# Six edits to a two-layer hybrid backbone: raw merge gates, weights' low parts ahead of the masks, gate matmuls between row transposes, squares added on VectorE, a shorter rotary

## Chip, cores and metric

The kernel runs on one core of a Trainium2 chip. The metric is device time in microseconds (us) of one execution; several executions are taken and their median is compared.

## What is computed

Two layers over 512 tokens of 1024 features (256 context tokens, then 256 latent ones); batch 1; all in float32. Layer 1 needs its context only as keys and values, so most of its work covers the 256 latent tokens.

```python
h  = rms_norm(x, g1) * (1 + sc) + sh          # modulation from c, by w_mod
p  = split(h @ w_in)                          # mLSTM | MLA | NA | three gates of 1024
y_a = mlstm(p)      # 4 heads x 2 directions, log-sigmoid gates, sums and maxima along time
y_b = mla(p)        # 8 heads, 64 plain + 32 rotary features, RMS-normed q and k
y_c = natten(p)     # 8 heads, windowed with a bias, plus the context
y  = (sigmoid(ga)*y_a + sigmoid(gb)*y_b + sigmoid(gc)*y_c) @ w_out
x  = x + g1 * y
x  = x + g2 * (square(relu(rms_norm(x) mod @ w_ff1)) @ w_ff2)
```

A sigmoid is taken as (1 + tanh(z/2)) / 2, where z is the output of the gate projection.

## The kernel before

**Precision.** Every weight and every activation of a large product is split in a high part and a low part (high by ScalarE, L832 for weights; low = raw - high by GpSimd, L693 and L695, or by VectorE, L1253, for a fixed share of the blocks). A product is three matmuls: high x high, low x high, high x low. Weights stream by SyncE's DMA into a raw buffer and pass through a ring of high and low places. `reach(n)` (L479) gives the block up to which places are free once block n has been used; `ahead(n)` (ScalarE, L837), `low_to(reach(n))` (GpSimd, L700) and `share_ahead(n)` (VectorE, L1244) make the parts up to there. Each engine runs its instructions in the order in which the program issues them, so the place of these calls in each engine's code is the schedule.

**Order of a layer.** Norm; the mLSTM's projection (blocks `ml`, seven); the mLSTM; neighbourhood attention (`na`); the latent attention (`mla`); the merge of three gated branches; output projection (`wo`); norm; the feed-forward pair (`ff`, 32 steps). The 24 tiles of the gate projections (`gate`, each 24 matmuls, L1881) are spread as filler: `chain` tiles while VectorE works on the mLSTM's scans, eight `loop` tiles in the loop over heads and directions, `last` tiles behind it, others (`cn`, `units`) in the preparation of the latent attention. `FILL` (L152) says how many where; `pump(tile, n)` (L1887) issues n matmuls of a tile.

**Gates.** `gate_out` (ScalarE, L843) takes a finished tile from its bank: with Tanh for the tiles before the `units` part, with Copy for those (`untouched`, L156). Some go to DRAM and come back by SyncE (`load_gate`, L571). `normed` (L965) needs a logarithm and an exponential for each head; ScalarE loads a function table where the next function is not in the one that it holds. `branch_out` (VectorE, L1540) multiplies 1 + tanh with a branch's output tile; in the latent attention two buffers (`side_tanh`) hold gates in turn.

**mLSTM.** After the last projection TensorE transposes small rows (L2009, L2014; L1370 and L1372 are VectorE's copies between them) and runs the chain tiles. VectorE computes for both directions (L1377 to L1399, four partitions wide) the gate sums and maxima by scans (L1389, L1392, L1394), and TensorE turns the result back (L2021, L2022). In the loop over `it` (L2060, 8 turns: 4 heads x 2 directions) it broadcasts a maximum (`broadcast_max`, L2030) for the next turn, which needs ScalarE's exponentials of this one (L962), runs 12 and 12 matmuls of a gate tile around the next head's scores (L2042), then, once GpSimd's mask (L731) is there, the products with the values (L2078). GpSimd's code is mask 0, low parts, mask 1, low parts, and so on. The last head is turned (L2053) after the last but one of the `last` tiles.

**Attentions.** Two heads or rows in each step s: VectorE takes the maxima (L1679), ScalarE the exponentials with their sums (L1136), VectorE or GpSimd divides (L1656, L763), TensorE transposes (L2228), ScalarE copies (L1155), TensorE multiplies with the values. Between these run the branch projection's matmuls (L1907). `rope` (L1327) is the rotary part: a multiply with the cosine (L1335), four small ones with the sine (L1339), an addition (L1341); a small copy (L1606) signals that a query block is done.

**Norm.** ScalarE squares each of eight chunks of the residual stream (L879); TensorE sums all of them over the partitions by a float32 matmul with ones (L1946, `square_sum`), two behind each residual chunk pair; ScalarE takes Ln and Exp (L891, L892); VectorE and ScalarE make the normed chunks, and the next projection begins (L1863).

```python
low_to(reach(N["ml", l, 6]))                       # GpSimd, ahead of the loop
for hd in range(2 * ML_H):
    pool.wait_ge(*S(f"ml{l}_P").at(hd + 1))
    pool.affine_select(...)                        # the mask, L731
    low_to(reach(N["gate", l, hd]))
```

## Time and profile before

| | us |
|---|---|
| median of three runs | 1687.56 (1683.96 to 1689.25) |
| the profiled execution, its own time | 1691.04 |
| its span, first to last instruction | 1689.3 |
| TensorE busy | 1576.3 |
| VectorE busy | 1000.5 |
| ScalarE busy | 757.5 |
| GpSimd busy | 691.4 |
| mean granted clock of TensorE | 0.970 of full |

The profiled execution is one more execution, taken with the hardware profiler. PE is TensorE, DVE is VectorE, ACT is ScalarE, POOL is GpSimd, SP is SyncE. A busy TensorE is not one at its peak, and the idle time of an engine off the bounding path costs nothing. Where several operations follow at one line, the timeline shows them as one row with their count.

### The profile page before, as it was taken

To read this page: it belongs to the slowest core of one execution; us is meant where nothing else is said; L and a number is where in the kernel's file an instruction comes from. 1 tells how busy PE (TensorE), PEld (TensorE's weight loads), DVE (VectorE), ACT (ScalarE), POOL (GpSimd) and SP (SyncE) were. 2 spreads that over 40 slices of the span, in tenths; PEclk is the share of its full clock that TensorE was granted. 3 is DMA by queue.
4 is the path that set the end of the run, shared out by engine and by line. 5 is a ranking of instruction groups with operands and counts; after the bars stand their busy time and mean duration, and the time that the engine had idled before them with its cause. 6 is when DMAs were issued, how large, how long until landed. Compare 5 with 4: busy or idle time off the path is not lost.

```text
span 1689.3 us, 24992 instructions
## 1 busy us (share of the span) xinstructions
PE 1576.3 (93%) x9728; PEld 1341.6 (79%) x9728; DVE 1000.5 (59%) x1737; ACT 757.5 (45%) x1506; POOL 691.4 (41%) x407
## 2 busy tenths in 40 slices
PE   7897998989999999899999998979898989989998
PEld 3776778967877687688888886967897876889998
DVE  5755934875367762668696964144127287665554
ACT  4424653455544643523232334347436545554443
POOL 0451324634343012455554543534455453234442
PEclk9998999999999999999999998989999999999999
DMA  8442434421225132243455742132520343435553
GB/s 328 185 183 81 181 113 150 151 100 53 83 100 193 26 128 97 75 159 122 169 199 193 279 151 100 69 100 81 162 101 26 122 144 101 157 129 192 179 178 122
DMA packets 69852, 230.64 MB, mean 137 GB/s; under 512 B 18280, under 2 KB 24808, under 8 KB 56424
## 3 DMA queue, kind: packets, MB, share of 16 engines
q1 hardware_dynamic: 60880, 213.67, 35.7%
q10 hardware_dynamic: 8856, 15.39, 2.5%
q8 instruction: 77, 1.26, 0.3%
q14 instruction: 39, 0.32, 0.1%
HBM read 216.45 MB, written 12.58 MB: 136 GB/s over the span
## 4 chain that ended last, share of the span: by engine, by line
PE 77%; DVE 9%; ACT 6%; POOL 4%; issue 3%; DMA 1%; ACTq 0%; DVEq 0%
PE bank L1843 39%; PE bank L1925 10%; PE bank L1881 8%; PE bank L1863 4%; PE bank L1907 3%; PE bank L2228 2%; PE bank L2204 2%; PE bank L2215 2%; POOL wL L693 1%; ACT wH L832 1%; POOL wL L695 1%; PE bank L2078 1%; DVE arena L1339 1%; DVE mjunk L1268 1%; PE bank L1946 1%
## 5 line engine op out<-in xcount | busy, mean ns | idle before, releaser
L695 POOL TENSOR_TENSOR wL<-raw,wH 128x768 fp32r<-128x768 f32 (+3 forms) x198 | 327.7, 1655 | 354.5 <-ACT wH L832 354.4
L832 ACT ACTIVATE wH<-raw 128x768 fp32r<-128x768 f32 (+6 forms) x396 | 296.9, 807 | 387.4 <-PE bank L1843 287.3
L693 POOL TENSOR_TENSOR wL<-raw,wH 128x1280 fp32r<-128x1280 f32 (+2 forms) x144 | 298.8, 2075 | 413.3 <-ACT wH L832 413.3
L1843 PE MATMUL bank<-hH,wH 128*128 128x512 f32 (+1 forms) x720 | 247.8, 344 | 2.4 <-POOL wL L695 1.5
L1843 PE MATMUL bank<-hH,wL 128*128 128x512 f32 (+1 forms) x720 | 244.6, 340 | 0.0
L1843 PE MATMUL bank<-hL,wH 128*128 128x512 f32 (+1 forms) x720 | 244.5, 340 | 0.0
L1843 PE MATMUL bank<-oH,wH 128*128 128x512 f32 (+1 forms) x576 | 194.5, 338 | 0.5 <-issue 0.5
L1843 PE MATMUL bank<-oH,wL 128*128 128x512 f32 (+1 forms) x576 | 193.6, 336 | 0.0
L1843 PE MATMUL bank<-oL,wH 128*128 128x512 f32 (+1 forms) x576 | 193.6, 336 | 0.0
L1271 DVE SCALAR_TENSOR_TENSOR acc<-acc,cb 128x1024 f32<-128x1024 f32 x88 | 167.2, 1914 | 2.5
L1881 PE MATMUL bank<-hH,wH 128*128 128x512 f32 (+1 forms) x384 | 138.8, 362 | 18.0 <-POOL wL L695 11.7
L1843 PEld LDWEIGHTS bank<-hH,wH 128*128 128x128 f32 x720 | 136.5, 190 | 19.9 <-POOL wL L695 2.1
L1843 PEld LDWEIGHTS bank<-hL,wH 128*128 128x128 f32 x720 | 136.6, 190 | 16.0 <-issue 1.2
L1843 PEld LDWEIGHTS bank<-hH,wL 128*128 128x128 f32 x720 | 136.5, 190 | 15.3
L1925 PE MATMUL bank<-wH,hH 128*128 128x256 f32 x480 | 138.9, 289 | 9.5 <-POOL wL L695 9.3
L1925 PE MATMUL bank<-wL,hH 128*128 128x256 f32 x480 | 137.7, 287 | 0.0
L1925 PE MATMUL bank<-wH,hL 128*128 128x256 f32 x480 | 137.6, 287 | 0.0
L1881 PE MATMUL bank<-hL,wH 128*128 128x512 f32 (+1 forms) x384 | 132.5, 345 | 0.0
L1881 PE MATMUL bank<-hH,wL 128*128 128x512 f32 (+1 forms) x384 | 132.4, 345 | 0.0
L1760 DVE SCALAR_TENSOR_TENSOR arena<-bank,modT,arena 128x256 f32<-128x256 f32 x120 | 54.1, 480 | 130.5 <-PE bank L1843 125.9
L1843 PEld LDWEIGHTS bank<-oH,wH 128*128 128x128 f32 x576 | 109.3, 190 | 12.5 <-issue 1.4
L1843 PEld LDWEIGHTS bank<-oL,wH 128*128 128x128 f32 x576 | 109.4, 190 | 11.6 <-issue 0.5
(213 smaller groups left out, 3140.7 us busy)
## 6 DMA issues: line engine op xcount, KB each, us to landing
raw<-in_p_ff SPq DMA_DIRECT2D x64, 1024.0 KB, 4.8
acc<-in_p_mod SPq DMA_DIRECT2D x44, 1024.0 KB, 5.4
raw<-in_p_ml SPq DMA_DIRECT2D x12, 1024.0 KB, 5.0
raw<-in_p_na SPq DMA_DIRECT2D x12, 1024.0 KB, 4.9
raw<-in_p_mgc SPq DMA_DIRECT2D x16, 512.0 KB, 3.5
raw<-in_p_mga SPq DMA_DIRECT2D x16, 512.0 KB, 3.5
raw<-in_p_mgb SPq DMA_DIRECT2D x16, 512.0 KB, 3.6
raw<-in_p_out SPq DMA_DIRECT2D x8, 1024.0 KB, 4.8
```

Of the source, the lines that this page charges most:

```text
L693: pool.tensor_tensor(l_[:, 0:cut], r_[:, 0:cut], h_[:, 0:cut].bitcast(F32), ALU.subtract)
L695: pool.tensor_tensor(l_[:, cut:k * w], r_[:, cut:k * w], h_[:, cut:k * w].bitcast(F32), ALU.subtract)\
L832: act.activation(flat(wH, n)[:, part], flat(raw, n)[:, part], ACT.Copy)\
L1271: ins = dve.scalar_tensor_tensor(row, row, 1.0, cb[:, last, :], ALU.mult, ALU.mult, accum_out=modT[:, l, chunk, last:last + 1])
L1760: ins = dve.scalar_tensor_tensor(x[:, c + b, lo:lo + 256], src[:, lo:lo + 256], modT[:, l, gate + c + b, s:s + 1], x[:, c + b, lo:lo + 256 ...
L1843: ins = pe.matmul(dst, w_[:, kk, c:c + P], r_[:, kk, lo:TOK], start=kk == k0 and m == 0, stop=kk == k0 + kn - 1 and m == 2)
L1863: ins = pe.matmul(dst, w_[:, kk, c:c + P], r_[:, kk, lo:TOK], start=kk == 0 and m == 0, stop=kk == KC - 1 and m == 2)
L1881: ins = pe.matmul(bank[gate_bank(l, T)][:, t0:TOK], w_[:, kk, :], r_[:, kk, t0:TOK], start=kk == 0 and m == 0, stop=kk == KC - 1 and m == 2)
L1907: ins = pe.matmul(bank[2 + T % 2][:, t0:TOK], w_[:, kk, :], r_[:, o + kk, t0:TOK], start=kk == 0 and m == 0, stop=kk == 3 and m == 2)
L1925: ins = pe.matmul(bk[:, o:o + width], s_[:, at[kk], t * P:t * P + P], w_[:, kk, c:c + width], start=kk == 0 and m == 0, stop=kk == k - 1 a ...
L2204: pe.matmul(bank[4 + i][:, 0:nk], l_q[0:MLA_D, 2 * g + i, t * P:t * P + P], l_k[0:MLA_D, 2 * g + i, 0:nk], start=True, stop=True).then_inc ...
L2215: ins = pe.matmul(bank[s % 2][64 * i:64 * i + 64, 0:P], v_[:, c, h * 64:h * 64 + 64], s_pt[:, i, c * P:c * P + P], start=c == 0, stop=c == ...
```

## The change

- `gate_out` always copies. The tanh is taken in the attentions by ScalarE (`branch_tanh`), in place, one step before `branch_out` needs it; `branch_out` waits for it. The reload of the logarithm's table in `normed` is taken out.
- GpSimd makes low parts up to the reach of the last chain tile before the first mask, and after mask hd those of the loop tile one turn earlier (none after mask 0).
- The first chain tile uses bank 2 and is issued in pieces: 5 matmuls (8 in layer 1) before the row transposes of L2009, 4 (6) before those of L2014, the rest behind. Layer 1 has four chain tiles and two last ones. In turn 0 of the loop twelve matmuls of the tile go ahead of `broadcast_max(1)`.
- ScalarE and VectorE make parts of the next weights in turns 9 and 10, before they end the last head.
- In the later three norms VectorE adds chunks 1 to 5 onto chunk 0, and TensorE sums three: that total, chunk 6, chunk 7. The first norm (0,0) stays as it was.
- `rope` multiplies with the sine in two instructions instead of four, and its last instruction signals in place of the small copy. In layer 1 ScalarE makes the next query weights' high parts before it loads the square root's table.
- The first biased pair of layer 1 is divided by VectorE instead of GpSimd.

```diff
@@ -150,12 +150,7 @@
 FILL = (dict(chain=3, loop=8, last=3, cn=2, units=(1, 1, 1, 1, 1, 1, 1, 1)),
-        dict(chain=3, loop=8, last=3, cn=2, units=(2, 2, 1, 1, 1, 1)))
-def untouched(l, T):
-    return T >= gate_range(l, 0).start
+        dict(chain=4, loop=8, last=2, cn=2, units=(2, 2, 1, 1, 1, 1)))
...
@@ -273,7 +268,7 @@
     pairs = head_pairs(l)
-    return biased(br, pairs[s][1]) and s < len(pairs) - 1
+    return biased(br, pairs[s][1]) and 0 < s < len(pairs) - 1
...
@@ -524,13 +527,17 @@
+        def branch_step(br, l, c):
+            return max(side_step(br, l, c) + 1, 3 if (br, l) == ("na", 0) else 0)
             if T in gate_range(l, "chain"):
-                return T
+                return (2, 0, 1, 3)[T]
...
@@ -722,7 +729,7 @@
                 pool.memset(m_v[:, :, :, ML_DV:ML_DV + 1], 1.0).then_inc(S(f"ml{l}_zero").handle, 1)
-                low_to(reach(N["ml", l, 6]))
+                low_to(reach(N["gate", l, gate_range(l, "chain").stop - 1]))
...
@@ -731,7 +738,8 @@
                         .then_inc(S(f"ml{l}_mask").handle, 1)
-                    low_to(reach(N["gate", l, hd]))
+                    if hd:
+                        low_to(reach(N["gate", l, gate_range(l, "loop")[hd - 1]]))
...
@@ -849,17 +857,13 @@
                         act.wait_ge(*S("mod_done").at(len(PAIRS)))
-                    act.activation(g_acc[:, c, t0:], bk, ACT.Tanh, scale=0.5).then_inc(S("gate_free").handle, 1)
+                    act.activation(g_acc[:, c, t0:], bk, ACT.Copy).then_inc(S("gate_free").handle, 1)
                         act.wait_ge(*S(f"gate_out{n % 2}").at(16 * before))
-                    if untouched(l, T):
-                        ins = act.activation(gst[:, n % 2, t0:], bk, ACT.Copy)
-                    else:
-                        ins = act.activation(gst[:, n % 2, t0:], bk, ACT.Tanh, scale=0.5)
-                    ins.then_inc(S("gate_free").handle, 1)
+                    act.activation(gst[:, n % 2, t0:], bk, ACT.Copy).then_inc(S("gate_free").handle, 1)
...
@@ -874,9 +878,15 @@
                 tag = f"nrm{l}{which}_"
-                if c >= 2:
-                    act.wait_ge(*S(tag + "sum").at(c - 1))
-                act.activation(n_sq[:, c % 2, t0:TOK], x[:, c, t0:TOK], ACT.Square).then_inc(S(tag + "sq").up(1), 1)
+                if (l, which) == (0, 0):
+                    if c >= 2:
+                        act.wait_ge(*S(tag + "sum").at(c - 1))
+                    dst = n_sq[:, c % 2, t0:TOK]
+                else:
+                    if c >= 3:
+                        act.wait_ge(*S(tag + "add").at(c - 2))
+                    dst = square_of(c)[:, t0:TOK]
+                act.activation(dst, x[:, c, t0:TOK], ACT.Square).then_inc(S(tag + "sq").up(1), 1)
...
@@ -968,7 +978,6 @@
                         link(ins)
-                    exp_and_ln()
...
@@ -988,6 +997,8 @@
                         normed(h)
+                    if it == 2 * ML_H + 1:
+                        ahead(N["gate", l, gate_range(l, "last")[-2]])
...
@@ -1036,6 +1047,8 @@
                         gates_out(l, "cn")
+                        if l == 1:
+                            ahead(N["uq", l, 0])
...
@@ -1123,6 +1136,25 @@
+                    def branch_tanh(c):
+                        if br == "mla":
+                            act.wait_ge(*S(f"gate_in{c % 2}").at(16 * (KC // 2 * l + c // 2 + 1)))
+                            raw_gate = side_tanh[:, c % 2, t0:]
+                        else:
+                            if l == 0:
+                                act.wait_ge(*S(f"gate_a{c // 4}").at(16 * KC // 2))
+                            else:
+                                act.wait_ge(*S("gate_free").at(GATES * l + TURN.index((0, c)) + 1))
+                            raw_gate = g_acc[:, c, t0:]
+                        act.activation(raw_gate, raw_gate, ACT.Tanh, scale=0.5).then_inc(S(tag + "tanh").up(1), 1)
+                    def branch_tanhs(s):
+                        for c in range(KC):
+                            if max(branch_step(br, l, c) - 1, 0) == s:
+                                branch_tanh(c)
...
@@ -1138,8 +1170,12 @@
                     for s in range(len(turns) + 2):
+                        if br == "na":
+                            branch_tanhs(s)
                             exponentials(s)
+                        if br == "mla":
+                            branch_tanhs(s)
...
@@ -1333,12 +1369,11 @@
                 dve.tensor_tensor(t1, src, over(cos), ALU.mult)
-                for part in range(2):
-                    for hf in range(2):
-                        o, w = part * 16 + hf * 8, part * 16 + (1 - hf) * 8
-                        ins = dve.tensor_tensor(t2[:, :, o:o + 8], src[:, :, w:w + 8], over(sin[:, o:o + 8]), ALU.mult)
+                halves = [v.rearrange("p g (a h w) -> p g a h w", a=2, h=2) for v in (t2, src, over(sin))]
+                for hf in range(2):
+                    ins = dve.tensor_tensor(halves[0][:, :, :, hf, :], halves[1][:, :, :, 1 - hf, :], halves[2][:, :, :, hf, :], ALU.mult)
                 link(ins)
-                link(dve.tensor_tensor(dst, t1, t2, ALU.add))
+                return dve.tensor_tensor(dst, t1, t2, ALU.add)
...
@@ -1470,6 +1505,8 @@
                                                  m_o[:, h, t0:], ALU.mult, ALU.mult).then_inc(S(tag + "y").up(1), 1)
+                    if it == 2 * ML_H + 2:
+                        share_ahead(N["gate", l, gate_range(l, "last")[-2]])
...
@@ -1542,15 +1579,11 @@
                         src = bank[2 + T % 2][:, t0:TOK]
+                        dve.wait_ge(*S(tag + "tanh").at(c + 1))
                         if br == "na":
-                            if l == 0:
-                                dve.wait_ge(*S(f"gate_a{c // 4}").at(16 * KC // 2))
-                            else:
-                                dve.wait_ge(*S("gate_free").at(GATES * l + TURN.index((0, c)) + 1))
                         else:
-                            dve.wait_ge(*S(f"gate_in{c % 2}").at(16 * (KC // 2 * l + c // 2 + 1)))
...
@@ -1599,11 +1632,11 @@
                             if is_q:
-                                link(dve.tensor_tensor(r, r, ropeg[:, l, 0:1, :].broadcast_to([P, G, ROPE]), ALU.mult))
+                                ins = dve.tensor_tensor(r, r, ropeg[:, l, 0:1, :].broadcast_to([P, G, ROPE]), ALU.mult)
                                 if t >= 2:
-                                    rope(r, r, l_r, t - 2, G)
-                                dve.tensor_copy(stat[0:1, 60:61], stat[0:1, at + 8:at + 9]).then_inc(S(tag + "st").up(1), 1)
+                                    link(ins)
+                                    ins = rope(r, r, l_r, t - 2, G)
+                                ins.then_inc(S(tag + "st").up(1), 1)
...
@@ -1750,6 +1783,16 @@
+                def add_squares(l, which, t0, cs):
+                    tag = f"nrm{l}{which}_"
+                    for c in cs:
+                        dve.wait_ge(*S(tag + "sq").at(c + 1))
+                        if c >= 2:
+                            dve.wait_ge(*S(tag + "add").at(c - 1))
+                        dve.tensor_tensor(n_sq[:, 0, t0:], n_sq[:, 0, t0:], square_of(c)[:, t0:], ALU.add)\
+                            .then_inc(S(tag + "add").up(1), 1)
...
@@ -1766,6 +1809,8 @@
                     residual(u0 + j, 2 * j, M_GATE1)
+                    if j < 3:
+                        add_squares(l, 1, t0, range(max(1, 2 * j), 2 * j + 2))
...
@@ -1791,6 +1836,8 @@
                             residual(u, 2 * (j - 4), M_GATE2)
+                            if (l, i) == (0, 3) and j < 7:
+                                add_squares(1, 0, 0, range(max(1, 2 * j - 8), 2 * j - 6))
...
@@ -1936,9 +1983,15 @@
-            def square_sums2(l, which, t0, c):
-                for b in range(2):
-                    square_sum(l, which, t0, c + b)
+            def squares_total(l, which, t0):
+                tag = f"nrm{l}{which}_"
+                pe.wait_ge(*S(tag + "add").at(KC - 3))
+                pe.matmul(bank[4][:, t0:TOK], ones, n_sq[:, 0, t0:TOK], start=True, stop=False).then_inc(S(tag + "sum").up(1), 1)
+                for c in (6, 7):
+                    pe.wait_ge(*S(tag + "sq").at(c + 1))
+                    pe.matmul(bank[4][:, t0:TOK], ones, square_of(c)[:, t0:TOK], start=False, stop=c == 7)\
+                        .then_inc(S(tag + "sum").up(1), 1)
...
@@ -2004,18 +2057,26 @@
                     filled(ins, u0 + 6, b)
+                pe.wait_ge(*S("bank_free2").at((u0 + 5) // 2 + 1))
+                first_gate = gate(l, 0, 0)
+                pump(first_gate, 5 if l == 0 else 8)
                 ins.then_inc(S(tag + "turned").up(1), 1)
+                pump(first_gate, 4 if l == 0 else 6)
                     ins.then_inc(S(tag + "rows").up(1), 1)
-                gates(l, "chain")
+                pump(first_gate, 25)
+                for T in gate_range(l, "chain")[1:]:
+                    pump(gate(l, T, 0), 25)
                     pe.wait_ge(*S(tag + "nmrow").at(d + 1))
+                    if l == 1:
+                        pe.wait_ge(*S("gate_free").at(GATES * l + gate_range(l, "chain").stop))
...
@@ -2060,6 +2121,8 @@
                     tile = gate(l, T, GATES * l + T)
+                    if it == 0:
+                        pump(tile, 12)
...
@@ -2243,11 +2306,9 @@
                 features(n0 + 1, u0 + 1, KC, both(KC, t0), hH, hL)
-                square_sums2(l, 1, t0, 0)
                     features(n0 + j, u0 + j, KC, both(KC, t0), hH, hL)
-                    square_sums2(l, 1, t0, 2 * j - 2)
-                square_sums2(l, 1, t0, 6)
+                squares_total(l, 1, t0)
...
@@ -2261,10 +2322,8 @@
                                      (lambda kk: S(f"ff{l}_hid").at(i * 8 + kk + 1)) if j == 4 else None)
-                        if l == 0 and i == 3 and j > 4:
-                            square_sums2(1, 0, 0, 2 * (j - 5))
                 if l == 0:
-                    square_sums2(1, 0, 0, 6)
+                    squares_total(1, 0, 0)
...
```

## Rows read from the trace of the kernel before

**Rows 1.** The page, busy us of each engine, share of the span, instructions.
```profile
PE 1576.3 (93%) x9728; PEld 1341.6 (79%) x9728; DVE 1000.5 (59%) x1737; ACT 757.5 (45%) x1506; POOL 691.4 (41%) x407
...
PE 77%; DVE 9%; ACT 6%; POOL 4%; issue 3%; DMA 1%; ACTq 0%; DVEq 0%
```

**Rows 2.** Waits of TensorE over the span: line, releaser, total us, times, longest.
```profile
PE bank L1881 <- POOL wL L695: 11.7, 5, 5.7
PE bank L1925 <- POOL wL L695: 11.5, 4, 4.8
...
PE bank L2155 <- DVE stat L1606: 7.0, 4, 2.2
PE bank L2228 <- POOL arena L763: 6.7, 6, 5.0
...
PE bank L1881 <- ACT gst L861: 3.6, 3, 1.3
PE bank L1881 <- ACT acc L852: 2.7, 2, 1.3
...
PE bank L2053 <- ACT arena L977: 2.2, 3, 1.1
...
PE bank L2009 <- DVE arena L1370: 1.9, 2, 0.9
...
PE bank L2014 <- DVE small L1372: 1.0, 2, 0.5
```

**Rows 3.** Timeline of TensorE, layer 0: start, us, instruction, idle before and releaser.
```profile
142.18 0.22 PE L2021 MATMUL bank<-const,arena 4*128 4x4 f32 x1
...
148.96 1.10 PE L2030 MATMUL bank<-arena,const 128*128 128x512 f32 x2 [2.63 <-ACT arena L962]
155.76 0.79 PE L1881 MATMUL bank<-hH,wH 128*128 128x512 f32 x1 [5.71 <-POOL wL L695]
...
257.98 0.55 PE L1925 MATMUL bank<-wH,hH 128*128 128x256 f32 x1 [4.27 <-POOL wL L695]
```

**Rows 4.** Timeline of GpSimd, the first mask of layer 0.
```profile
150.67 0.63 POOL L731 TENSOR_SCALAR_AFFINE_SELECT arena<-arena 128x512 f32<-128x512 f32 x1 [28.16 <-DVE arena L1422]
```

**Rows 5.** Timeline of VectorE, first and last of 12 scan operations, layer 0.
```profile
129.29 0.68 DVE L1383 SCALAR_TENSOR_TENSOR arena<-arena 4x512 f32<-4x512 f32 x1 [1.42 <-ACT arena L948]
...
138.44 0.68 DVE L1399 SCALAR_TENSOR_TENSOR arena<-arena 4x512 f32<-4x512 f32 x1
```

**Rows 6.** Timelines of VectorE and GpSimd, the rotary of layer 0.
```profile
464.51 0.49 DVE L1339 TENSOR_TENSOR arena<-arena,const 128x32 f32<-128x32 f32 x4
...
468.50 4.08 DVE L1339 TENSOR_TENSOR arena<-arena,const 128x32 f32<-128x32 f32 x4
...
468.40 1.60 POOL L693 TENSOR_TENSOR wL<-raw,wH 128x640 fp32r<-128x640 f32 x1
```

**Rows 7.** Groups by line and shape, ScalarE: count, busy us, mean ns, idle before.
```profile
L861 ACT ACT_TABLE_LOAD x9 | 11.5, 1283 | 0.2
L861 ACT ACTIVATE gst<-bank 128x512 f32<-128x512 f32 x16 | 9.5, 593 | 25.2 <-PE bank L1881 24.7 <-ACT gst L861 0.5
```

**Rows 8.** Timeline of TensorE, layer 1, the wait for the scans.
```profile
1125.99 0.22 PE L2021 MATMUL bank<-const,arena 4*128 4x4 f32 x1 [4.09 <-DVE arena L1399]
```

**Rows 9.** Timeline of TensorE, the second norm of layer 0.
```profile
670.65 2.50 PE L1946 MATMUL bank<-arena,const 128*128 128x512 f32 x5
674.43 1.13 PE L1946 MATMUL bank<-arena,const 128*128 128x512 f32 x2 [1.29 <-ACT arena L879]
```

**Rows 10.** Windows: PE, PEld, DVE, ACT, POOL busy us (count), clock, DMA share, GB/s.
```profile
176.00:195.00 19.00, 17.58 (x92) 13.49 (x91) 17.12 (x33) 12.64 (x35) 9.13 (x8) 1.00 0.58 213
1127.00:1142.00 15.00, 11.74 (x51) 9.00 (x52) 3.32 (x10) 4.65 (x14) 5.75 (x6) 0.56 0.26 77
```

**Rows 11.** Waits of ScalarE from 336 to 440 us, neighbourhood attention of layer 0.
```profile
ACT arena L1136 <- DVE stat L1679: 15.6, 8, 3.7
```

**Rows 12.** Window on L1881 alone, a loop tile of layer 1: PE, PEld busy, clock, DMA, GB/s.
```profile
1135.00:1140.44 5.44, 5.41 (x24) 5.19 (x24) 0.52 0.51 137
```

More of the change, by code:

```diff
@@ L507, in first_biased, with divisions_by_pool @@
             return next(s for s, (_, t, _) in enumerate(head_pairs(l)) if biased("na", t))
+        def divisions_by_pool(br, l, s):
+            return sum(divided_by_pool(br, l, k) for k in range(s))
         def scaled_by_dve(br, l, s):
@@ L888, in norm @@
                 tag = f"nrm{l}{which}_"
-                act.wait_ge(*S(tag + "sum").at(KC))
+                act.wait_ge(*S(tag + "sum").at(KC if (l, which) == (0, 0) else 3))
                 link(act.activation(n_std[:, t0:TOK], bank[4][:, t0:TOK], ACT.Ln, scale=1.0 / D, bias=eps[:, 0:1]))
```

16 lines of the change are left out of this document (9 added, 7 removed).

## Prediction, before the changed kernel was run

> **What bounds the kernel now.** I read the page's busy row and chain first. TensorE is busy 1576.3 of 1689.3 us and holds 77% of the chain; the rest of the chain is other engines standing in for it [rows 1]. So a microsecond counts only if it closes one of TensorE's gaps (113 us in all), removes a matmul, or gives back a stretch at the lower clock. The second view, the waits of TensorE by releaser, names the gaps [rows 2]: weights' low parts from POOL (11.7 us before gate tiles, 11.5 before projections), DVE's rotary (7.0), POOL's division (6.7, one wait 5.0 of it), and, behind ACT's table loads, gate copies and head copies (3.6, 2.7, 2.2). The third, timelines, shows why each is there. After the masks' first turn in layer 0 TensorE stands 2.63 us for the exponentials and then 5.71 us for a low part [rows 3]; POOL had been idle for 28.16 us before that mask, since its program order puts the low part behind it [rows 4].
>
> **The change part by part.** Sums are against the profiled execution, 1691.0 us (span 1689.3 and 1.7 around it).
>
> *Low parts ahead of the mask.* The two waits in the loop of layer 0 and two of layer 1 go: 11.7 less 0.6 that belongs to the attention preparation, 11.1 us. TensorE runs at 0.56 of its clock from 1127 to 1142, with 11.74 us busy there [rows 10]; the 24 matmuls of one gate tile take 5.41 us in it [rows 12]. With the waits after it gone I take back 2.5 us over both layers (0 to 6).
>
> *Its price.* The lows now run beside DVE's scans (first at 129.29, last ending 139.12; 12 operations, of which 10 read two tensors from SBUF) [rows 5], where POOL was idle. The nearest row for that meeting is the rotary's: four small multiplies take 0.49 us alone and 4.08 beside low parts, 0.9 us more for each, and 1.60 is the POOL operation they stood behind [rows 6]. In layer 0 two tiles' lows (four operations) fit in: 3.6 us (0 to 6.4). The chain ended 3.1 us before TensorE came to it at 142.18 [rows 3, 5]; with 1.5 us of that used by the next part, 2.0 us are lost. In layer 1 five tiles' lows are free to run and eight scan operations are still to come: 8 x 0.9 = 7.2 us (0 to 12.8), all on the path, as TensorE already waits 4.09 us there [rows 8]. The Trainium skill (SBUF — State Buffer, section "Who interferes with whom") speaks against this change in the same way: a VectorE instruction with two SBUF inputs and a GpSimd instruction that reads SBUF exclude each other for the whole instruction. By it both terms stand at their full size; by a reading in which POOL's rows are only slow by themselves they would be 0 and the forecast 9.2 us lower. The rotary rows agree with the rule.
>
> *Gate tile between the row transposes, 12 matmuls ahead of the second maximum.* The tile is cut into the waits on L1370 and L1372 (1.9 and 1.0 us for both layers) [rows 2]. Half of that, 1.5 us, counts in layer 0; in layer 1 it only lengthens the wait for the scans, 0. The 2.63 us before the second maximum [rows 3] are filled by twelve matmuls that ran afterwards anyway: 2.6 us.
>
> *Gates kept raw.* ACT's loop no longer switches between tanh and the logarithm's set: L861 alone has nine loads of 1.28 us [rows 7]. The gaps behind them, 3.6 + 2.7 + 2.2 = 8.5 us [rows 2], go. The 16 tanhs per layer that move to the attentions (about 0.59 us each on ACT where 512 wide, as its copy of a gate tile is [rows 7]) meet an ACT that waits 15.6 us for DVE's maxima in the neighbourhood attention of layer 0 alone [rows 11]. A branch_out of DVE now waits for a tanh set one step before, and the exponentials and output copies of ACT stand behind the gate's DMA: I charge 2 us (0 to 8).
>
> *Last head.* Low and high parts of the attention's first weights start before the head is turned: 4.27 us [rows 3] go in layer 0. In layer 1 the wait is the 4.8 of [rows 2]; I let 3.0 go, since one tile fewer covers it, and that tile (half of 5.41 [rows 12], 2.7 us) moves into the scans' wait: 10.0 us together.
>
> *Squares on DVE.* TensorE stands 1.29 us between the sums for ScalarE's last square [rows 9], and longer behind the last sum. Five records of the sum took 2.50 us; a sum is two records. Of eight sums three stay: 5 x 0.86 = 4.3 us less work, and 0.6 of the 1.29. That is 4.9 us for each of two norms 512 wide and half for the third: 12.1 us (6 to 13). The standard deviation and all behind it is unchanged, so the wait behind the sums stays. Cost on DVE nothing on the path: its adds lie beside feature matmuls.
>
> *Rotary.* Two multiplies and a copy less in each. Beside POOL that is 2 x 0.9 + 0.14 us, alone 0.3. The waits on L1606 (7.0) shrink to about 1.4; with high parts of the queries started before the table load in layer 1, 2.4 of low-part waits and the 0.6 mostly go too, with 1 us of clock: 8.5 us (4 to 11).
>
> *Division of the first pair in layer 1 by DVE*: the wait of 5.0 us becomes about 1.2, DVE's own maximum and exponential: 3.8 us (3 to 5).
>
> *What is late next.* In the middle of the loop of layer 0 DVE is busy 17.12 of 19 us and TensorE 17.58 [rows 10]: with gaps closed, DVE's modulation columns stand close to the bound. I charge 4 us (0 to 12).
>
> **Sum.** 11.1 + 2.5 + 1.5 + 2.6 + 8.5 + 10.0 + 12.1 + 8.5 + 3.8 = 60.6; less 2.0 + 7.2 + 2 + 4 = 15.2; 45.4 us. 1691.0 - 45.4 = 1645.6, and the median of the runs shown (1687.56) is 3.5 us under the profiled one: **1642 us**. Without any of the charges it would be 1627.
>
> **The rivals.** *DVE becomes the bound of the loop.* Charges at their upper ends in the loop (12 instead of 4, 6.4 and 12.8 instead of 3.6 and 7.2): 8 + 2.8 + 5.6 = 16.4 us more, 1658 us. For it: the 17.12 of 19 above and the 4.08; against: L1271 and its like read SBUF and are met by POOL already now.
>
> *The table loads stay*, since a set without tanh or copy is loaded elsewhere: the change would not do what it says. 8.5 us and 1.5 of clock stay, 1652 us. Against: tanh, copy and exponential run in the merge without a load between them.
>
> *Slower: the masks held behind low parts.* POOL is one queue; after each mask it must now finish lows that reach further than before, and each waits for a high part, that for a place that TensorE frees and for a load. Where that takes longer than a head's time, the next mask is late and TensorE's products with it. A low of two POOL operations is some 2.7 us; with the high ahead of it about 4 us late for each of 14 masks, 56 us: 1642 + 56 = 1698 us. It decides from the point where the weights' loads run less than one head ahead. Against it: every mask now is released by DVE, after POOL idled 28.16 us before the first [rows 4].
>
> **Chances.** Forecast 0.64, DVE-bound loop 0.18, table loads 0.08, masks 0.05; 0.05 is left for a mixture near no change. The range reaches from the sum without charges to some way above the DVE rival: 1625 to 1668. A measurement of this kernel tells 0.3%, 5 us, from no change; the cases give faster 0.90, within 0.04, slower 0.06.
>
> **What the profile after would show.** Right: the table loads of L861 gone; POOL lows between 1118 and 1132 and scans of 1.5 us and more beside them; TensorE waiting some 10 us for L1399 in layer 1 and 2 to 3 in layer 0; no wait on POOL before loop tiles; six records of the sum at each later norm; DVE's L1606 gone. Wrong: waits on masks or on tanh in TensorE's or ACT's list, a scan chain of unchanged 9.8 us (then the time is nearer 1633), or waits on L1422 or L1432 in the loop in the place of the table loads' (then 1658).

## Result and the profile after the change

The changed kernel takes 1632.03 us (median; 1631.35 to 1633.33), the kernel before 1687.05 in the same comparison: a ratio of 0.9677, 95% interval 0.9664 to 0.969. Faster was forecast, at 1642 us, with a range of 1625 to 1668. The gain is 55 us where the sum gave 45.

The page of the changed kernel, busy us by engine and the chain (answering to [rows 1]):

```profile
PE 1550.2 (95%) x9698; PEld 1325.1 (81%) x9698; DVE 1025.6 (63%) x1717; ACT 742.7 (46%) x1518; POOL 694.1 (43%) x406
...
PE 73%; DVE 12%; ACT 5%; issue 4%; POOL 3%; DMA 2%; SPq 0%; ACTq 0%; POOLq 0%; DVEq 0%
```

TensorE's idle time fell from 113.0 us (1689.3 - 1576.3) to 81.4 us (1631.6 - 1550.2), 31.6 us less; its busy time fell by 26.1 us. Of that some 10 us are matmuls taken out (15 sums). The rest was not taken apart; most of it fits the clock, whose mean granted value rose from 0.970 to 0.979 (as an estimate, 1566 us x (1 - 0.970/0.979) = 14 us).

The waits of TensorE in the changed kernel (answering to [rows 2]; L1928 is a gate tile's matmul, L1972 a projection, L2218 the transposes behind the rotary, L2291 those behind the division, L2082 those behind the scans, L2114 the head's turn):

```profile
PE bank L2082 <- DVE arena L1434: 7.2, 2, 6.0
PE bank L2218 <- DVE arena L1376: 5.5, 5, 1.6
...
PE bank L1972 <- POOL wL L702: 3.3, 4, 1.3
PE bank L2291 <- POOL arena L771: 2.2, 6, 0.7
...
PE bank L1928 <- POOL wL L702: 2.0, 1, 2.0
...
PE bank L1928 <- ACT gst L866: 0.6, 1, 0.6
PE bank L2114 <- ACT arena L986: 0.6, 1, 0.6
PE bank L2082 <- ACT gst L866: 0.6, 1, 0.6
```

In each of these lists the numbers are the total in us, the times and the longest. Gate tiles wait 2.0 us for low parts instead of 11.7, and 0.6 for ACT's copies instead of 6.3. One wait grew, as forecast: that for the scans, from 4.1 to 7.2 us. VectorE and GpSimd beside each other in layer 1 show why:

```profile
1083.95 1.21 DVE L1424 TENSOR_TENSOR_SCAN arena<-arena 4x512 f32<-4x512 f32 x1
1085.20 0.74 DVE L1432 SCALAR_TENSOR_TENSOR arena<-bank,bias,arena 4x512 f32<-4x512 f32 x1
1085.97 1.94 DVE L1424 TENSOR_TENSOR_SCAN arena<-arena 4x512 f32<-4x512 f32 x1
1087.95 1.30 DVE L1434 SCALAR_TENSOR_TENSOR arena<-arena 4x512 f32<-4x512 f32 x1
1089.28 1.95 DVE L1418 SCALAR_TENSOR_TENSOR arena<-arena 4x512 f32<-4x512 f32 x1
...
1098.71 1.84 DVE L1434 SCALAR_TENSOR_TENSOR arena<-arena 4x512 f32<-4x512 f32 x1
...
1085.27 1.57 POOL L700 TENSOR_TENSOR wL<-raw,wH 128x640 fp32r<-128x640 f32 x1 [9.00 <-ACT wH L840]
1086.79 1.91 POOL L702 TENSOR_TENSOR wL<-raw,wH 128x384 fp32r<-128x384 f32 x1
1088.67 2.01 POOL L700 TENSOR_TENSOR wL<-raw,wH 128x640 fp32r<-128x640 f32 x1
```

The same L1424 takes 1.21 us until GpSimd starts at 1085.27 and 1.94 after it; L1434 takes 1.30 and 1.84 where it took 0.68 [rows 5]. GpSimd's operations are stretched too (1.91 for 1.0). The operation that reads a bank, L1432, keeps its 0.74. The scans last from 1083.24 to 1100.55, 17.3 us instead of 9.8; in layer 0, with two tiles' lows beside them, 12.6.

**Where the gain lies, by stage.** Start of the same TensorE instruction in both traces, and the terms of the sum by stage:

| up to | before | after | gained in the stage | forecast |
|---|---|---|---|---|
| first broadcast maximum, layer 0 | 143.71 | 143.35 | 0.4 | -0.5 |
| neighbourhood projection, layer 0 | 257.98 | 240.38 | 17.2 | 14.1 |
| latent attention's query projection, layer 0 | 479.83 | 459.42 | 2.8 | -1.0 |
| layer 1's mLSTM projection L1925 | 1067.84 | 1034.75 | 12.7 | 11.8 |
| first broadcast maximum, layer 1 | 1127.03 | 1102.01 | -8.1 | -7.2 |
| neighbourhood projection, layer 1 | 1203.94 | 1158.50 | 20.4 | 16.6 |
| second query projection, layer 1 | 1354.19 | 1301.15 | 7.6 | 6.1 |
| side projection in latent attention, layer 1 | 1406.29 | 1349.55 | 3.7 | 3.2 |
| end | 1689.3 | 1631.6 | 1.0 | 2.4 |

The last but one row is in part luck: up to 1.6 of its 3.7 us are a wait of TensorE (1.9 us, at 1369 in the kernel before, 0.3 in the changed one) that no edit was meant to close, and that comes and goes in the experiments below.

### The profile page after: what moved, and what is told of

It reads as the page before. It is cut to its first block, busy times and chain, and to the rows that moved or that the text cites. A ratio compares the mean times of both kernels' runs of the same rounds, so it can differ in the third digit from the quotient of the medians.

```text
span 1631.6 us, 24934 instructions
## 1 busy us (share of the span) xinstructions
PE 1550.2 (95%) x9698; PEld 1325.1 (81%) x9698; DVE 1025.6 (63%) x1717; ACT 742.7 (46%) x1518; POOL 694.1 (43%) x406
## 4 chain that ended last, share of the span: by engine, by line
PE 73%; DVE 12%; ACT 5%; issue 4%; POOL 3%; DMA 2%; SPq 0%; ACTq 0%; POOLq 0%; DVEq 0%
PE bank L1890 39%; PE bank L1972 9%; PE bank L1928 7%; PE bank L1910 4%; PE bank L1954 3%; PE bank L2291 2%; PE bank L2267 2%; ACT wH L840 2%; PE bank L2278 2%; DVE mjunk L1304 2%; DVE acc L1307 2%; POOL wL L700 1%; PE bank L2141 1%; POOL arena L771 1%; ACT arena L1168 1%
## 5 line engine op out<-in xcount | busy, mean ns | idle before, releaser
L700 POOL TENSOR_TENSOR wL<-raw,wH 128x1280 fp32r<-128x1280 f32 (+2 forms) x144 | 299.0, 2076 | 429.6 <-ACT wH L840 429.4
L702 POOL TENSOR_TENSOR wL<-raw,wH 128x768 fp32r<-128x768 f32 (+3 forms) x198 | 331.1, 1672 | 342.9 <-ACT wH L840 342.8
L1972 PE MATMUL bank<-wH,hH 128*128 128x256 f32 x480 | 137.1, 286 | 3.7 <-POOL wL L702 3.3
L1928 PE MATMUL bank<-hH,wH 128*128 128x512 f32 (+1 forms) x384 | 137.0, 357 | 2.7 <-POOL wL L702 2.0
L1972 PE MATMUL bank<-wH,hL 128*128 128x256 f32 x480 | 136.0, 283 | 0.0
L1972 PE MATMUL bank<-wL,hH 128*128 128x256 f32 x480 | 136.0, 283 | 0.0
L1928 PE MATMUL bank<-hH,wL 128*128 128x512 f32 (+1 forms) x384 | 131.1, 341 | 0.0
L1928 PE MATMUL bank<-hL,wH 128*128 128x512 f32 (+1 forms) x384 | 130.7, 340 | 0.0
L1890 PEld LDWEIGHTS bank<-oH,wH 128*128 128x128 f32 x576 | 109.4, 190 | 12.2 <-issue 1.0
L1890 PEld LDWEIGHTS bank<-oH,wL 128*128 128x128 f32 x576 | 109.4, 190 | 11.2
L1890 PEld LDWEIGHTS bank<-oL,wH 128*128 128x128 f32 x576 | 109.4, 190 | 11.1
```

What stands on the lines that cost most here:

```text
L700: pool.tensor_tensor(l_[:, 0:cut], r_[:, 0:cut], h_[:, 0:cut].bitcast(F32), ALU.subtract)
L702: pool.tensor_tensor(l_[:, cut:k * w], r_[:, cut:k * w], h_[:, cut:k * w].bitcast(F32), ALU.subtract)\
L1890: ins = pe.matmul(dst, w_[:, kk, c:c + P], r_[:, kk, lo:TOK], start=kk == k0 and m == 0, stop=kk == k0 + kn - 1 and m == 2)
L1928: ins = pe.matmul(bank[gate_bank(l, T)][:, t0:TOK], w_[:, kk, :], r_[:, kk, t0:TOK], start=kk == 0 and m == 0, stop=kk == KC - 1 and m == 2)
L1972: ins = pe.matmul(bk[:, o:o + width], s_[:, at[kk], t * P:t * P + P], w_[:, kk, c:c + width], start=kk == 0 and m == 0, stop=kk == k - 1 a ...
```

## Experiments

Each is set against the changed kernel's median of 1632.0 us. The kernel before ran beside each experiment, and its median moved: 1687.0 us for experiments 1 to 4, 1689.4 for 5, 6, 8 and 9, 1686.4 for 7 and 10, 1687.4 for 11 and 12, against 1687.05 for the changed kernel. So a difference of medians can be off by 2 us. The table sets beside it what the ratios to the kernel before say (ratio less 0.9677, times 1687 us; the two intervals together leave 3.3 to 4.0 us either way) and the difference of the profiled spans (from 1631.6 us).

| experiment | by medians | by ratios | by profiled spans |
|---|---|---|---|
| 1, lows off the scans | -7.5 | -7.4 | -6.5 |
| 2, lows spread | -4.5 | -4.6 | -7.8 |
| 4, tanh in gate copies | 14.2 | 14.2 | 13.0 |
| 5, eight sums | 12.2 | 9.4 | 11.2 |
| 6, long rotary | 4.7 | 2.2 | 3.1 |
| 7, GpSimd divides | 7.1 | 6.2 | 5.9 |
| 8, no early pieces | 3.9 | 0.0 | 4.8 |
| 9, late parts | 7.3 | 4.2 | 6.0 |
| 10, old order of lows | 19.9 | 19.4 | 20.4 |

Experiments 6 and 8 are not clear of noise by their times; there the traces have to decide. "Aligned" below means that the same TensorE instruction is looked up in both traces. One difference at a single place needs care: between 1346 and 1351 us experiments 2 and 4 to 10 all fall back by 1.2 to 1.6 us against the changed kernel's trace, whatever their edit.

**1. Low parts kept off the scans.** The changed kernel, GpSimd waiting for the last scan operation behind the chain tiles' lows:

```diff
+                low_to(N["gate", l, gate_range(l, "chain").stop - 1] + 1)
+                pool.wait_ge(*S(f"ml{l}_nmrow").at(2))
                 low_to(reach(N["gate", l, gate_range(l, "chain").stop - 1]))
```

> The changed kernel, with GpSimd waiting for VectorE's last scan operation before it makes the low parts that reach past the chain tiles. Lock theory (a VectorE operation with two inputs in SBUF and a GpSimd low part shut each other out): the scans, 12.6 us in layer 0 and 17.3 us in layer 1 of the changed kernel, fall to 9.8 and to 9.8 to 11.5 (one tile's lows stay beside them in layer 1); TensorE's waits for them, 1.1 and 6.0 us, fall to 0 and 0 to 1; but the lows end later, the first mask with them, which costs 1 to 4. Time 1632 - 7 + 2 = 1627 us. Rival (the scans are longer for another reason, as the moved gate tile or the clock): scans stay at 12.6 and 17.3, and the later lows make it 1634 to 1638.

Measured: 1624.5 us (1623.96 to 1626.83), ratio to before 0.9633, interval 0.9616 to 0.9651. VectorE's timeline in layer 1, the scans from the third operation on:

```profile
1083.49 1.94 DVE L1426 TENSOR_TENSOR_SCAN arena<-arena 4x512 f32<-4x512 f32 x1
1085.47 1.30 DVE L1436 SCALAR_TENSOR_TENSOR arena<-arena 4x512 f32<-4x512 f32 x1
1086.81 0.68 DVE L1420 SCALAR_TENSOR_TENSOR arena<-arena 4x512 f32<-4x512 f32 x1
...
1091.27 0.68 DVE L1436 SCALAR_TENSOR_TENSOR arena<-arena 4x512 f32<-4x512 f32 x1
```

Only the two operations beside the one tile's low that stayed are long (1.94, 1.30); the others are back at 0.68. The scans last 11.2 us (1080.76 to 1091.95), in layer 0 9.8, and TensorE's wait for them is gone from the list. The price is the lows' later end: TensorE waits 0.69 us for mask 0 in layer 1. The lock theory holds, its rival falls; this version is faster than both kernels, by 7.5 us against the changed one (3.7 us either way).

**2. The same, with the lows spread around mask 0.**

```diff
+                low_to(N["gate", l, gate_range(l, "chain").stop - 1] + 1)
+                pool.wait_ge(*S(f"ml{l}_nmrow").at(2))
+                low_to(reach(N["gate", l, 0 if l == 0 else 1]))
...
                     if hd:
                         low_to(reach(N["gate", l, gate_range(l, "loop")[hd - 1]]))
+                    else:
+                        low_to(reach(N["gate", l, gate_range(l, "chain").stop - 1]))
```

> As the last one, but after the scans only the first few of these lows stand ahead of mask 0 and the rest behind it. Lock theory: both waits for the scans nearly gone as before, and mask 0 in time: 1632 - 7 = 1625 us. Rival (lows past the chain tiles have to be ready before mask 0): the gate tiles of the first loop turns wait for low parts, 3 us or more, and it is 1628 or above.

Measured: 1627.5 us (1625.49 to 1628.06), interval 0.9631 to 0.9669; its profiled span was 1623.8, that of experiment 1 1625.1, so the two cannot be told apart with certainty. TensorE's list shows a new wait of 2.2 us, in layer 0 at 159 us, for VectorE's products that become the mask's input (L1461):

```profile
PE bank L2107 <- DVE arena L1461: 2.2, 1, 2.2
```

Nothing was won over experiment 1, though mask 0 is no longer held. The rival's waits for low parts did not come either: those before gate tiles stay at 2.0 us, as in the changed kernel.

**3. The new order of low parts alone, in the kernel before.**

```diff
-                low_to(reach(N["ml", l, 6]))
+                low_to(reach(N["gate", l, gate_range(l, "chain").stop - 1]))
...
-                    low_to(reach(N["gate", l, hd]))
+                    if hd:
+                        low_to(reach(N["gate", l, gate_range(l, "loop")[hd - 1]]))
```

> The kernel before with the new order of GpSimd's low parts alone. Theory: the waits of 5.7, 1.4, 3.2 and 0.8 us before loop tiles go (11.1, and 1 to 3 of clock), the scans of layer 1 grow by 5 to 7 us on the path, those of layer 0 by 2.7 beside gate tiles that cover 3.1: 1687 - 7 = 1680 us. Rival (no lock on the path): 1687 - 13 = 1674. Second rival (lows ahead of masks hold masks back): no faster than 1687.

Measured: 1679.8 us (1674.56 to 1685.46), interval 0.9943 to 0.9978. Its waits:

```profile
PE bank L2022 <- DVE arena L1400: 9.8, 2, 9.1
...
PE bank L1882 <- ACT gst L862: 4.9, 4, 1.3
...
PE bank L2054 <- ACT arena L978: 3.0, 4, 1.1
```

Those on low parts before loop tiles are gone from the list (11.7 before). The wait for the scans is 9.1 us in layer 1 instead of 4.1, and the waits behind table loads are longer (4.9 and 3.0 for 3.6 and 2.2): part of what the lows gave went into them. Alone the edit is worth 7.3 us by the medians and 6.6 by the ratio, which leaves 3.7 to 9.6; the ten executions lie far apart. The second rival (no faster) falls; the first (1674 us) is just outside the interval, and the wait of 9.1 us speaks against it.

**4. Tanh back in the gate copies.**

```diff
-                    act.activation(gst[:, n % 2, t0:], bk, ACT.Copy)
+                    if untouched(l, T): ins = act.activation(gst[...], bk, ACT.Copy)
+                    else: ins = act.activation(gst[...], bk, ACT.Tanh, scale=0.5)
...
+                    exp_and_ln()                        # in normed
...
-                        branch_tanhs(s)
```

> The changed kernel with the tanh back in gate_out, the logarithm's table loaded again for each head, and no tanh in the attentions. Theory: the gaps behind table loads come back, 8.5 us, and 1 to 2 of clock; the attentions give back nothing since the tanhs there were hidden: 1632 + 10 = 1642 us. Rival (the tanhs cost the attentions 2 us or more): 1632 + 10 - 2 to 5 = 1637 to 1640, with attentions shorter by so much. Second rival (with low parts in time the loads are covered): 1632 to 1635.

Measured: 1646.2 us (1644.66 to 1648.85), interval 0.9743 to 0.9779: 14.2 us more than the changed kernel, where 10 were expected. Its waits and its table loads:

```profile
PE bank L2124 <- ACT arena L996: 4.9, 5, 1.9
...
PE bank L1938 <- ACT acc L865: 4.0, 3, 1.3
PE bank L1938 <- ACT gst L874: 3.9, 3, 1.3
```

```profile
L886 ACT ACT_TABLE_LOAD x16 | 20.5, 1283 | 0.3
L874 ACT ACT_TABLE_LOAD x8 | 10.3, 1283 | 0.1
L865 ACT ACT_TABLE_LOAD x4 | 5.1, 1283 | 0.1
```

The waits behind ACT are 12.8 us, not the 8.5 of [rows 2]: with low parts in time, ACT's 1.28 us loads are next in line and bare. Aligned with the changed kernel by equal TensorE instructions, this one falls back by 9.0 us between the second maximum of layer 1 and the last head's turn, and by some 4 us in the loop of layer 0. In the attentions of layer 0 it gains some 2 us back, of which 1 us is a difference that experiment 6, which has the tanhs, shows at the same place (336 us); in layer 1 it gains nothing back. So the tanhs cost about 1 us, in layer 0.

**5. Eight sums on TensorE again** (`square_sums2` behind each chunk pair, no `add_squares`).

```diff
-                squares_total(l, 1, t0)
+                square_sums2(l, 1, t0, 6)               # and (0), (2), (4) behind their chunks
```

> The changed kernel with all eight squares of each norm summed by TensorE again. Theory: five sums more in each of three norms and the longer wait between them, 4.9 + 4.9 + 2.4 = 12 us: 1644 us. Rival (only the sums behind the last feature tile count, the others lay in waits of TensorE): 5 to 8 us, 1637 to 1640.

Measured: 1644.2 us (1642.86 to 1644.95), interval 0.9718 to 0.9747: 12.2 us by the medians, 9.4 by the ratio. The end of the second norm of layer 0 in the changed kernel:

```profile
645.40 1.02 PE L1993 MATMUL bank<-arena,const 128*128 128x512 f32 x2
647.38 1.12 PE L1993 MATMUL bank<-arena,const 128*128 128x512 f32 x2 [0.96 <-ACT arena L889]
...
653.20 0.76 PE L1910 MATMUL bank<-hH,wH 128*128 128x512 f32 x1 [4.70 <-DVE hL L1344]
```

Against [rows 9] there are fewer sums and the wait between them is 0.96 for 1.29; the 4.70 behind them is what stays. Aligned with the changed kernel, this one falls back by 5.0 us in each of the two norms 512 wide, so there the full price of the matmuls counts and the rival (only the last sums) falls. In the third norm, 256 wide, it falls back by about 0.3 us and not by 2.4: TensorE waits 1.50 us for ScalarE's last square there with either form. The three norms account for 10.3 of the 11.2 us between the profiled spans.

**6. The long rotary again.**

```diff
-                for hf in range(2): ...                 # two multiplies
+                for part in range(2):
+                    for hf in range(2): ...             # four
...
-                                ins.then_inc(S(tag + "st").up(1), 1)
+                                link(ins)
+                                dve.tensor_copy(stat[0:1, 60:61], ...).then_inc(S(tag + "st").up(1), 1)
```

> The changed kernel with four sine multiplies and the trailing copy again. Theory: two multiplies more stand behind low parts of GpSimd, 0.9 us each, in the blocks that TensorE waits for: 1 to 1.5 us for each of four such blocks, 5 us: 1637 us. Rival (the waits that remain are set by GpSimd's lows or by the norm of the block, not by the rotary): under 2 us, 1632 to 1634.

Measured: 1636.7 us (1635.37 to 1638.81), interval 0.969 to 0.9705: 4.7 us by the medians, 2.2 by the ratio, so the time alone does not rule out the rival. The wait is 8.7 us where the changed kernel has 5.5, 3.2 us more; its releaser is the small copy at the end of the long rotary:

```profile
PE bank L2220 <- DVE stat L1641: 8.7, 5, 2.2
```

**7. GpSimd divides the first biased pair of layer 1 again** (`s < len(pairs) - 1` without `0 <`).

> The changed kernel with the first biased pair of layer 1 divided by GpSimd again. Theory: the wait of 5.0 us for L763 of the kernel before comes back in place of one of 1.3: 3.7 to 4.6 us, 1636 us. Rival (with the rest of the layer earlier GpSimd is free in time): under 1 us, 1632 to 1633.

Measured: 1639.1 us (1638.16 to 1639.7), interval 0.9695 to 0.9733: 7.1 us by the medians, 6.2 by the ratio, more than either theory. The profile divides it:

```profile
PE bank L2291 <- POOL arena L771: 7.0, 6, 5.0
```

```profile
PE bank L1972 <- issue: 1.9, 1, 1.9
```

5.0 us for the division have replaced 1.3, and TensorE runs slowly behind it: from 1228.5 to 1235.5 us its granted clock is 0.51, with 32 matmuls, where the changed kernel has 84 in the same 7.0 us (1229.9 to 1236.9) at 1.00. Aligned, the experiment falls back by 5.6 us between 1158 and 1240 us: the wait's 3.7 and 1.9 behind it. That slow stretch is what the theory left out. The second fence is from the preparation of the latent attention in layer 1: a wait of 1.9 us that is 0.3 in the changed kernel's profile. The kernel before and experiments 3 and 8 have it too, and experiments 1, 5 and 6 do not, so it comes and goes with how the engines meet; what decides it was not tried. It explains little of the difference: aligned, from 1299 to 1346 us the experiment falls back by 0.8 us in all, since other waits there are shorter.

**8. No early pieces of gate tiles** (the three `pump` calls taken out).

```diff
-                pump(first_gate, 5 if l == 0 else 8)
...
-                pump(first_gate, 4 if l == 0 else 6)
...
-                    if it == 0:
-                        pump(tile, 12)
```

> The changed kernel without the pieces of the first gate tile between the row transposes and without the twelve matmuls ahead of the second maximum; four chain tiles in layer 1 stay. Theory: 2.6 us for the maximum in layer 0 and about 1 in layer 1 come back; of the pieces nothing, since the scans set the end in both layers once GpSimd's lows run beside them: 1632 + 3.5 = 1635.5 us. Rival (the pieces count at their full 1.5 us in layer 0): 1637 us.

Measured: 1635.9 us (1632.26 to 1638.16), interval 0.9658 to 0.9697: 3.9 us by the medians, and 0.0 by the ratio, 0.9677 as for the changed kernel. The time shows no difference that is clear of noise. The waits of the trace show where the edit acts:

```profile
PE bank L2080 <- DVE arena L1434: 7.5, 1, 7.5
...
PE bank L2089 <- ACT arena L972: 2.4, 1, 2.4
```

The maximum's 2.4 us is back. Aligned, this kernel is 2.9 us behind the changed one just after it in layer 0, of which 1.8 are left at the neighbourhood attention, and 1.4 us further behind after the second maximum of layer 1. Up to the end of the scans of layer 0 the two are level (0.1 us): the wait for the scans in layer 0 is gone and the one in layer 1 longer, so the transposes' pieces had only moved time into it.

**9. Parts of the last head's turns made late again.**

```diff
-                    if it == 2 * ML_H + 1:
-                        ahead(N["gate", l, gate_range(l, "last")[-2]])
...
-                    if it == 2 * ML_H + 2:
-                        share_ahead(N["gate", l, gate_range(l, "last")[-2]])
```

> The changed kernel without the early high and low parts of the last head's turns. Theory: the 4.3 us wait before the neighbourhood attention's projection in layer 0 comes back with 2.2 us of half clock behind it, and 3 us or more in layer 1: 1632 + 9.5 = 1641.5 us. Rival (the wait came from other work that has gone, raw gates and table loads): under 4 us, below 1636.

Measured: 1639.3 us (1635.11 to 1641.81), interval 0.9684 to 0.972: 7.3 us by the medians, 4.2 by the ratio. The waits before projections are 6.2 us for 3.3:

```profile
PE bank L1968 <- POOL wL L702: 6.2, 3, 3.1
```

Less than the 9.5 expected: the waits that came back are about 3 us each (2.9 and 3.2), not 4.3 and 4.8. Aligned, the experiment falls back by 3.8 us around the one in layer 0; in layer 1 it falls back by 3.5 us and has all but 1.7 of it back at the end of that projection, where the changed kernel has waits of its own. The rival (under 4 us) is not excluded by the ratio; against it stand the two waits.

**10. The old order of low parts in the changed kernel** (with three chain and three last tiles in layer 1, which this order needs).

> The changed kernel with GpSimd's old order of low parts and, since this order needs it, three chain tiles and three last ones in layer 1; all else as changed. Theory (the parts of the change add up): the waits before loop tiles come back, 11 us and 1 to 3 of clock, the scans give back 1.1 + 7.5 less what a chain tile fewer leaves bare, the tail of layer 1 gets its tile of 2.9 again: 1632 + 12 - 7 + 3 = 1640 us. Rival (alone the order brought 7.3 us to the kernel before; it was worth more in the presence of raw gates, since table loads then no longer stand in the same places): 1644 to 1648, with waits for low parts longer than 5.7 us. Second rival (it is worth nothing without the lock avoided): 1632 to 1634.

Measured: 1652.0 us (1650.83 to 1653.66), interval 0.9775 to 0.9809. It is 19.9 us slower than the changed kernel; none of the theories went so far. TensorE and GpSimd in layer 0:

```profile
152.29 0.77 PE L1927 MATMUL bank<-hH,wH 128*128 128x512 f32 x1 [7.53 <-issue]
...
169.84 0.80 PE L1927 MATMUL bank<-hH,wH 128*128 128x512 f32 x1 [5.54 <-POOL wL L702]
```

```profile
149.10 0.64 POOL L738 TENSOR_SCALAR_AFFINE_SELECT arena<-arena 128x512 f32<-128x512 f32 x1 [26.69 <-DVE arena L1456]
149.71 1.53 POOL L700 TENSOR_TENSOR wL<-raw,wH 128x640 fp32r<-128x640 f32 x1
151.19 0.99 POOL L702 TENSOR_TENSOR wL<-raw,wH 128x384 fp32r<-128x384 f32 x1
```

The twelve gate matmuls now stand ahead of the second maximum, and they need the low that stands behind mask 0 (ready at 152.2). So the maximum, and with it the exponentials and the second mask, wait 7.5 us too, and a second wait of 5.5 us follows 12 us later. In layer 1 the same two waits are 4.4 and 2.6 us:

```profile
PE bank L1927 <- issue: 11.9, 2, 7.5
PE bank L1927 <- POOL wL L702: 8.2, 2, 5.5
```

Together they are 20.1 us, about the whole difference. Two edits of this change need each other: at that place of layer 0 the kernel before waited 2.6 + 5.7 us [rows 3], and the early pieces without the early lows wait 7.5 + 5.5.

**11 and 12. GpSimd beside the scans of the kernel before: reads, and writes alone.** Ten instructions in layer 1 from the start of the scans, results unused:

```diff
+                    pool.wait_ge(*S("ml1_ln").at(1))
+                    for n in range(10):
+                        pool.tensor_tensor(mjunk[:, 0:TOK], hH[:, 1, :], hH[:, 3, :], ALU.add)    # 11
+                        pool.memset(mjunk[:, :], 0.0)                                            # 12
```

> The kernel before, with ten GpSimd additions of two SBUF tensors (512 wide, results unused) beside the scans of layer 1, nothing else changed. Lock theory: the scans grow from 9.8 us by 6 to 9, as in the changed kernel, TensorE's wait of 4.1 us by as much, and the time is 1694 us. Rival (the scans are held by what the low parts bring with them, weights and DMA, or by nothing of GpSimd's): scans 9.8, time 1687.

> The same place, but ten GpSimd fills (1024 wide), which write SBUF and read nothing. Lock theory in its narrow form (only reads of GpSimd meet the second input of VectorE): scans 9.8 us and time 1687. Rival (any GpSimd instruction shuts out such a VectorE instruction): scans longer by 3 us or more, time 1690 or above.

Measured: with reads 1693.0 us (1690.53 to 1697.03), ratio 1.0034, interval 1.0022 to 1.0046; with writes 1688.3 us (1685.9 to 1689.9), ratio 1.0008, interval 0.9998 to 1.0017. VectorE with the reads beside it:

```profile
1114.85 2.20 DVE L1394 TENSOR_TENSOR_SCAN arena<-arena 4x512 f32<-4x512 f32 x1
1117.09 0.74 DVE L1402 SCALAR_TENSOR_TENSOR arena<-bank,bias,arena 4x512 f32<-4x512 f32 x1
...
1119.26 1.58 DVE L1404 SCALAR_TENSOR_TENSOR arena<-arena 4x512 f32<-4x512 f32 x1
```

and with the writes, which ran from 1113.80 for 10.05 us:

```profile
1114.48 1.21 DVE L1394 TENSOR_TENSOR_SCAN arena<-arena 4x512 f32<-4x512 f32 x1
...
1117.75 0.68 DVE L1404 SCALAR_TENSOR_TENSOR arena<-arena 4x512 f32<-4x512 f32 x1
...
1113.80 10.05 POOL L729 MEMSET mjunk<- 128x1024 f32 x10 [6.80 <-ACT arena L953]
```

The scans last 16.5 us (1114.13 to 1130.60) with reads and 9.8 (1113.77 to 1123.60) with writes. So it is GpSimd's reading of SBUF, not what the low parts bring with them, and only operations with both inputs in SBUF are met: L1402, which reads a bank, keeps its 0.74. The Trainium skill (SBUF — State Buffer, section "Who interferes with whom") says that a VectorE instruction with two SBUF inputs contends with a GpSimd instruction that reads SBUF and not with one that only writes it. Both halves agree with these runs, 16.5 us with reads and 9.8 with writes.

## Why the prediction was right, and where its sum was off

- **The lows' price beside the scans.** Forecast 3.6 us in layer 0 and 7.2 in layer 1; measured 2.7 (12.6 - 9.8) and 7.5 (17.3 - 9.8). The 0.9 us per operation taken from the rotary's rows was the right row. TensorE's waits for the scans are 1.1 and 6.0 us, where the prediction named 2 to 3 and some 10, and experiment 1 gets 7.5 back. Layer 1's is shorter since the fourth chain tile filled more of it than the 2.7 us counted: its matmuls took 4.6 us, with 2.0 us of wait for their low part ahead of them.
- **Waits on low parts in the loop.** Gone, as forecast. That they are worth 11.1 us whatever else is changed was wrong: the new order is worth 7.3 us alone (experiment 3, with the scans' longer wait in it) and 19.9 us beside the other edits (experiment 10). The steps are not independent.
- **Gates kept raw.** The term of 8.5 us was mis-sized, since it took the gaps that the trace showed behind loads that other waits were still covering. Taken out of the finished kernel the edit is worth 14.2 us. The 2 us charged for the tanhs were about 1.
- **The clock.** 2.5 us were taken back for both loops. Not priced at all was the stretch behind the wait before the neighbourhood projection of layer 0. The same 7.1 us of it, before and after:

```profile
257.90:265.00 7.10, 7.03 (x40) 7.06 (x41) 0.22 (x2) 1.49 (x2) 4.79 (x3) 0.64 0.53 170
```

```profile
240.30:247.40 7.10, 7.02 (x58) 7.05 (x59) 0.08 (x2) 2.45 (x4) 4.76 (x3) 1.00 0.46 170
```

  40 matmuls at a granted clock of 0.64, 58 at 1.00: 2.2 us of the third row of the stage table. Experiment 7 shows the same behind the division (1.9 us). Closing such a gap gives the gap and the slow stretch behind it. Not every gap has one: behind the 1.42 us at 178.55 in the loop of layer 0 the clock stayed at 1.00 [rows 10].
- **VectorE as the loop's bound**, charged at 4 us and given 0.18 as a rival: it did not come. Windows of the loop of layer 0 (and, below, of layer 1) after the change:

```profile
165.00:184.00 19.00, 19.00 (x107) 15.34 (x107) 18.59 (x40) 11.00 (x35) 8.29 (x6) 1.00 0.56 195
...
1108.00:1153.00 45.00, 44.80 (x359) 41.65 (x358) 21.89 (x77) 28.35 (x88) 17.97 (x19) 1.00 0.22 77
```

  TensorE is busy 19.00 of 19.00 us and VectorE 18.59: the bound stands 0.4 us away and is not reached. This 4 us, of which 3.1 show in the second row of the stage table, and the missing 2.2 of the clock are half of the 12 us by which the profiled gain (57.7) passes the sum; 3.8 more are in layer 1's loop, where raw gates count.
- **Squares.** 12.1 forecast (its terms add up to 12.25), 12.2 by the medians, 9.4 by the ratio. That the first two agree is luck. The two wide norms gave 5.0 us each for 4.9, with a sum nearer 0.94 than 0.86 us and 0.3 of the wait for 0.6; the third gave about 0.3 for 2.4.
- **Rotary and its weights.** 8.5 forecast. The term that let the waits on the rotary shrink from 7.0 to 1.4 was mis-sized: they are 5.5 in the changed kernel (L1376), less only in layer 0 (3.8 to 1.9) and in layer 1 no shorter than before (3.2 and 3.7). The rotary's own share is 3.2 by the waits of experiment 6, 4.7 by its median. The waits for low parts of 2.2 and 0.6 us in layer 1 are gone, as forecast; what the earlier high parts gave by themselves was not tried.
- **Last head.** 10.0 forecast with the moved tile; the early parts are worth 7.3 by the medians, 4.2 by the ratio.
- **Division.** 3.8 forecast; the wait shrinks by 3.7 us in the profile, and 1.9 more are the slow stretch behind it, which was priced at nothing; the medians differ by 7.1, the ratios by 6.2.
- **Pieces and maximum.** 2.6 + 1.5 forecast; 3.9 by the medians, which is not clear of noise, and by the traces 2.4 of the 2.6 and of the 1.5 nothing, since the scans set the end in both layers once the lows lay beside them.
- **The rivals.** Table loads stay: none is left at the gate copies. Masks held behind lows: TensorE's list has no wait on a mask.

The direction and most of the mechanism were right; the closeness of the total, 10 us off, is in part luck, since terms too small (raw gates, the clock behind two gaps) stand beside terms too large (the bound on VectorE, the rotary's waits, the third norm). The seven parts taken back one by one sum to 69.3 us by the medians (14.2 + 12.2 + 4.7 + 7.1 + 3.9 + 7.3 + 19.9) and to 55.6 by the ratios (14.2 + 9.4 + 2.2 + 6.2 + 0.0 + 4.2 + 19.4), where the whole change gave 55. So it is not shown that the parts together are worth more than the whole; it is shown for the order of the lows, 6.6 us alone and 19.4 with the rest by the ratios.

## What to carry to other kernels

Price a wait that several others cover by what it would be when they are gone, not by the gap that the trace shows now, and add the slow stretch behind a gap that is to close where the trace has one. When work is moved to an engine's idle time, look at what its partner in SBUF does in that time: here a GpSimd instruction that reads SBUF held a VectorE operation with two SBUF inputs for about the rest of that instruction (L1424 came 0.9 us before the end of L700's 1.57 and took 0.73 longer). Here the idle stretch chosen was a serial chain of such operations, and one wait that keeps the two apart gave 7.5 us. When small parts are taken back one by one, set each against the kernel before that ran beside it: here that kernel's own median moved by 2 us and more, as much as some of the parts are worth.

## What the runs showed of the hardware that was not expected

The exclusion stretches both sides (GpSimd's 1.00 us low part took 1.91 beside scans of 0.7 to 1.2), and in layer 1 the two engines' operations alternate one for one. GpSimd's fills leave the scans untouched to 0.01 us. An added 6.6 us on the scans of the kernel before moved its median by 5.5 us (1687.4 to 1693.0; the interval leaves 3.7 to 7.8).
